# A one-layer decoder trunk on one core: gather from centred rows, refills in row pieces, and the last normalisation split between the final block's tokens and all others

## The reference, cut to what matters

```python
x = LN(alpha*x + h)                      # 1: after the mixer
x = LN(alpha*x + MemCrossAttn(x, mem))   # 2: input of router and experts
x = LN(alpha*x + MoE_top4of32(x))        # 3: the output

def layer_norm(x, g, b):
    mu = mean(x); var = mean(square(x - mu))
    return (x - mu) * rsqrt(var + LN_EPS) * g + b

logits = x @ router_w + router_b         # 32 experts, the best 4 of each token
gate = softmax(top 4 logits)
expert(x) = clamped_swiglu(x @ w_gate[e] + b_gate[e], x @ w_up[e] + b_up[e]) @ w_down[e] + b_down[e]
y[token] += gate * expert(x[token])
```

## Time and profile before

| | us |
|---|---|
| median of 3 runs | 1213.64 |
| lowest, highest | 1211.48, 1213.74 |
| the profiled execution, its own time | 1215.79 |
| its span | 1213.8 |
| PE, DVE, ACT, POOL busy in it | 1058.9, 315.2, 187.9, 24.3 |
| moved from memory | 445.0 MB, mean 368 GB/s over the span |

### The profile page before, as it was taken

One profiled execution on the slowest core, in us unless ns is written; L12 is line 12 of the kernel. 1 busy time (PEld: TensorE's weight loads), 2 busy tenths in 40 slices (PEclk: granted clock), 3 DMA queues, 4 the chain that ended last, 5 costly groups with the idle time before them and its releaser, 6 DMA issues.

```text
span 1213.8 us, 19629 instructions
## 1 busy us (share of the span) xinstructions
PE 1058.9 (87%) x7607; PEld 488.7 (40%) x7608; DVE 315.2 (26%) x993; ACT 187.9 (15%) x434; POOL 24.3 (2%) x34
## 2 busy tenths in 40 slices
PE   9999999999879889989797979796969696978786
PEld 7776874964423333323232323232323232323232
DVE  1757433212412212222121212122112121212122
ACT  0221431120111111111010101111101010101012
POOL 0110010100000000000000000000000000000000
PEclk9999999999889999999898989898989898989898
DMA  9743240587799999999999999999999999999996
GB/s 349 278 165 139 71 173 9 209 339 328 302 430 431 427 432 430 433 431 433 431 432 432 432 431 432 432 427 437 424 438 431 431 432 431 431 430 431 431 425 281
DMA packets 34953, 446.40 MB, mean 368 GB/s; under 512 B 5920, under 2 KB 6384, under 8 KB 19184
## 3 DMA queue, kind: packets, MB, share of 16 engines
q1 hardware_dynamic: 31040, 442.30, 86.3%
q10 hardware_dynamic: 3888, 3.76, 0.9%
HBM read 445.00 MB, written 1.05 MB: 367 GB/s over the span
## 4 chain that ended last, share of the span: by engine, by line
PE 50%; DMA 41%; DVE 4%; issue 2%; DVEq 1%; ACTq 1%; ACT 1%; POOLq 0%; SPq 0%; POOL 0%; PEldq 0%
DMA main<-in_exp_w_down_dram 41%; PE bank L1585 12%; PE bank L1648 10%; PE bank L1021 5%; PE bank L1031 5%; PE bank L1415 2%; PE bank L1335 2%; PE bank L1487 2%; PE bank L1627 1%; PE bank L1104 1%; PE bank L1577 1%; ACTq L919 1%; DVEq L2166 1%; DVE kst L2172 1%; DVE main L2159 1%
## 5 line engine op out<-in xcount | busy, mean ns | idle before, releaser
L1585 PE MATMUL bank<-main 128*32 128x512 f32 x3008 | 360.7, 633 | 106.8 <-DMA main<-in_exp_w_up_dram 96.5
L1585 PEld LDWEIGHTS bank<-main 128*32 128x32 f32 x3008 | 112.6, 116 | 350.7 <-issue 345.4
L1648 PE MATMUL bank<-main,kst 128*32 128x512 f32 x1504 | 181.7, 598 | 30.9 <-DMA main<-in_exp_w_down_dram 18.9
L2159 DVE TENSOR_TENSOR main<-bank,main 128x256 f32<-128x256 f32 x94 | 39.6, 422 | 550.3 <-PE bank L1627 550.3
L1532 PE MATMUL bank<-main 64*128 64x512 f32 x384 | 95.6, 615 | 0.8 <-ACT main L969 0.8
L944 ACT ACTIVATE main<-bank 128x512 f32<-128x512 f32 x46 | 27.5, 598 | 418.5 <-PE bank L1585 418.1
L1648 PEld LDWEIGHTS bank<-main,kst 128*32 128x32 f32 x1504 | 40.4, 109 | 105.0 <-issue 79.2
L1031 PE MATMUL bank<-main 128*128 128x512 f32 x176 | 77.0, 593 | 0.0
L1021 PE MATMUL bank<-main 128*128 128x256 f32 x288 | 63.5, 380 | 0.0
L1021 PEld LDWEIGHTS bank<-main 128*128 128x128 f32 x288 | 54.3, 190 | 7.6 <-issue 0.3
L1487 PE MATMUL bank<-main,kst 128*32 128x256 f32 x752 | 53.0, 394 | 2.0 <-DVE kst L2063 2.0
(11 more groups left out here) (325 smaller groups left out, 768.0 us busy)
## 6 DMA issues: line engine op xcount, KB each, us to landing
main<-in_exp_w_up_dram SPq DMA_DIRECT2D x28, 4096.0 KB, 33.3
main<-in_exp_w_down_dram SPq DMA_DIRECT2D x28, 4096.0 KB, 38.6
main<-in_exp_w_gate_dram SPq DMA_DIRECT2D x36, 2048.0 KB, 26.0
main<-in_exp_w_gate_dram SPq DMA_DIRECT2D x14, 4096.0 KB, 40.8
main<-in_exp_w_up_dram SPq DMA_DIRECT2D x7, 2048.0 KB, 14.8
main<-in_exp_w_down_dram SPq DMA_DIRECT2D x7, 2048.0 KB, 13.8
main<-in_w_in_dram SPq DMA_DIRECT2D x5, 2048.0 KB, 22.9
main<-in_w_in_dram SPq DMA_DIRECT2D x8, 512.0 KB, 9.8
```

The costliest lines, as they stand in the source:

```text
L1585: last = pe.matmul(gu_bank[at:at + CAP, :], xg_chunk(k), hidden, start=(k == 0), stop=(k == KC - 1))
L1648: last = pe.matmul(y_bank[at:at + CAP, :], hT[:, j, f, :], row(role, j)[:, h * HALF:(h + 1) * HALF], start=(f == 0 and pair == 0), stop=(f ...
L2159: return tt(dst, gT[:, :, w, :, :], b.unsqueeze(3).broadcast_to([P, 4, 2, CAP]), ALU.add)
```

## The change

**Routing.** The router's products are turned: the router weights stand still in four groups of 32 columns and the tokens move (`rp0`, `rp1`), ACT copies the four partial sums, and one product with `router_pick` adds them (`logits`). Products of the identity with itself (`stay_busy`, written into banks not yet in use) are put between the waits. The first gather no longer takes normalised rows: rows 0 to 127 are centred, multiplied by the gain and by the root, rows 128 to 255 only centred and multiplied by the gain, with the root in the selection's weight (`spread_weight`); the shift `ln_b` is put in first by a product of ones (`gathered_shift`). The shift is added to `x3` later (`ln_ready` 3 and 4), and the four `begin_sum` come after the first block's gate and up products. The table of the order is computed ahead of `gate_up`.

**Refills.** D1 of position 1 comes in three pieces, each as soon as what lies under it is used: rows 2 and 3 after the router's products (`rp1`), row 0 when the last half is centred (`centred_ready` 3), row 1 after `ln_ready` 4. `G0` and `U0` of position 2 come in two pieces of two rows, the first after step 1 of `gate_up` (`rows_used`), the second after step 3.

**The end.** While the final block's weights arrive, the rows are normalised as if the final block added nothing (`base_rows` on DVE: statistics, eight passes over 128x512), with the root set to zero for rows that have a token in the final block (`kept`). For those tokens, at most 32, the closed sums are gathered into a 64x512 tile (`gather_rows`, one half of the columns in partitions 0 to 31, the other in 32 to 63), the block's result is added there with its gate multiplied in beforehand (`gated`, one more product of 128x256 on DVE), the statistics are taken on that tile and joined by two small products (`half_mean`, `half_gap`), the tile is scaled, and PE scatters it onto the sums, which have been opened with the normalised rows. What is left for the 256 rows is a copy out of PSUM. The gains of normalisation 3 are loaded as four rows of 2 KB and spread over the partitions by PE and ACT (`spread_gain`) instead of two broadcast loads.

PE's order near the first `gate_up`, before: L1474 and L1475 are the last of the counts, L1446 opens the second sum, L1487 is the gather, L1493 its transpose, L1585 `gate_up`, L1506 to L1510 the table.

The diff, cut to its core:

```diff
+            def load_rows(role, e, odd, first, n, arrived):
+                w = d[ROLE_INPUT[role]][0].rearrange("e (p h j) n -> e h p (j n)", h=2, j=4)
+                h = (0, 0, 1, 1, 0, 1)[role]
+                cols = slice(first * D_MODEL, (first + n) * D_MODEL)
+                at = weights_at(role, odd) + first * D_MODEL
+                src = w[bass.ds(e, 1), h, :, cols].rearrange("e p n -> p (e n)")
+                sp.dma_start(main[:, at:at + n * D_MODEL], src).then_inc(arrived, 16)
...
-            sp.wait_ge(ln_ready, 5)
-            load_role(D1, 1, odd=True)
+            sp.wait_ge(unit_filled, UNIT_AT["rp1"] + 1)
+            load_rows(D1, 1, True, 2, 2, ld_d1[0])
+            sp.wait_ge(centred_ready, 3)
+            load_rows(D1, 1, True, 0, 1, ld_d1[1])
             sp.wait_ge(order_ready, 1)
...
+            def refill_first():
+                done = blocks_through(0)
+                e = expert_at(0, 2)
+                sp.wait_ge(rows_used, done)
+                for i, role in enumerate((G0, U0)):
+                    load_rows(role, e, False, 0, 2, ld_refill[i])
+                sp.wait_ge(ln_ready, 4)
+                load_rows(D1, 1, True, 1, 1, odd_full[D1])
+                sp.wait_ge(gu0_used, done)
+                for role in (G0, U0):
+                    load_rows(role, e, False, 2, 2, ring_full[ROLE_SLOT[role]])
+                sp.wait_ge(gu_done, done)
+                load_role(G1, e, odd=False)
+                load_role(U1, e, odd=False)
+                sp.wait_ge(d0_used, done)
+                load_role(D0, e, odd=False)
+                sp.wait_ge(y_done, done)
+                load_role(D1, e, odd=False)
...
+            load_gain_rows()
             load_even(N_EXPERTS - 4, 2)
             load_halves(N_EXPERTS - 4, 3, odd=True, last=True)
-            sp.wait_ge(gu0_used, blocks_through(N_EXPERTS - 2))
-            sp.dma_start(ln3_g, d["ln3_g"][0:1, :].partition_broadcast(P)).then_inc(ld_ln, 16)
-            sp.dma_start(ln3_b, d["ln3_b"][0:1, :].partition_broadcast(P)).then_inc(ld_ln, 16)
...
+                for i in range(4):
+                    b, h = divmod(i, 2)
+                    act.wait_ge(sums_closed, i + 1)
+                    act.activation(x3[:, b, h * HALF:(h + 1) * HALF], acc[b][h][:, :], ACT.Copy).then_inc(sums_copied, 1)
+                for i in range(4):
+                    ps, h = (xgT_bank, xg_bank)[i % 2], i % 2
+                    act.wait_ge(spread_done, i + 1)
+                    if i < 2:
+                        act.activation(slot_gain[32 * h:32 * h + 32, :], ps[32 * h:32 * h + 32, :], ACT.Copy)
+                    act.activation((ln3_g, ln3_b)[i // 2][:, h * HALF:(h + 1) * HALF], ps[:, :], ACT.Copy).then_inc(gain_copied, 1)
...
             def route(ps, b, steps):
                 for k in steps:
-                    last = pe.matmul(ps[:, 0:N_EXPERTS], x2T[b][:, k, :], router_w3[:, k, :], start=(k == 0), stop=(k == KC - 1))
+                    c = k % 4
+                    last = pe.matmul(ps[32 * c:32 * c + 32, 0:P], router_w3[:, k, :], x2T[b][:, k, :], start=(k < 4), stop=(k >= 4))
                 return last
+            def logits(b):
+                need(f"rp{b}")
+                pe.matmul(begin(f"rt{b}")[:, 0:N_EXPERTS], router_parts[:, b, :], router_pick,
+                          start=True, stop=True).then_inc(unit_filled, 1)
...
+            route(begin("rp0"), 0, range(0, 8)).then_inc(unit_filled, 1)
             used_up(1, "wo3")
+            bank_rp1 = begin("rp1")
+            need("x2T2")
+            route(bank_rp1, 1, range(0, 4))
             need("wo3")
...
+            logits(0)
+            stay_busy(begin("rt1"), 2)
             pe.wait_ge(x2T3_first, 1)
-            route(ps, 1, range(4, 6))
+            route(bank_rp1, 1, range(4, 6))
             need("x2T3")
-            route(ps, 1, range(6, 8)).then_inc(unit_filled, 1)
...
+            bank_xg0 = begin("xg0")
+            pe.wait_ge(ld_ln, 64)
+            gathered_shift(bank_xg0)
+            stay_busy(begin("xgT0"), 2)
             pe.wait_ge(chosen, 1)
...
+                def gather_rows():
+                    for b in range(TB):
+                        for h in range(2):
+                            pe.wait_ge(sums_copied, 2 * b + h + 1)
+                            last = pe.matmul(xgT_bank[32 * h:32 * h + 32, :], selw[:, b, :], x3[:, b, h * HALF:(h + 1) * HALF],
+                                             start=(b == 0), stop=False)
+                    last.then_inc(rows_gathered, 1)
...
+                pe.wait_ge(y_copied, n + 1)
+                pe.wait_ge(gselT_ready, n + 1)
+                scatter(0, final=True)
+                scatter(1, final=True)
+                pe.wait_ge(ld_gain, 64)
+                spread_gain(0)
+                spread_gain(1)
+                for i in (2, 3):
+                    pe.wait_ge(gain_copied, i - 1)
+                    spread_gain(i)
+                pe.wait_ge(odd_full[G0], 8 * N_EXPERTS)
+                pe.wait_ge(odd_full[U0], 32)
+                for k in range(4):
+                    gate_up(k)
+                pe.wait_ge(gain_copied, 4)
+                gather_rows()
+                pe.wait_ge(gsel_ready, n + 1)
+                for b in range(TB):
+                    pe.matmul(gselT_bank[:, 256:256 + CAP], ones, gated[:, b, :], start=(b == 0), stop=(b == 1))
+                for b in range(TB):
+                    last = pe.transpose(gselT_bank[:, b * P:(b + 1) * P], gsel_rows[:, b, :], ident)
+                last.then_inc(gselT_done, 1)
...
+                pe.wait_ge(hT_ready, n + 1)
+                pe.wait_ge(odd_full[D0], 32)
+                for f, j in [(0, j) for j in range(4)] + [(1, 0), (1, 1)]:
+                    if f == 1 and j == 0:
+                        pe.wait_ge(last_down[0], 16)
+                    for h in range(2):
+                        last = down(y_bank, 64 * h + CAP * (j % 2), f, j, h, f == 0 and j < 2, f == 1)
+                last.then_inc(y_done, 1)
+                pe.wait_ge(last_down[1], 16)
+                for h in range(2):
+                    down(xgT_bank, 32 * h, 1, 2, h, False, False)
+                pe.wait_ge(y_copied, n + 2)
+                pe.matmul(xgT_bank[0:64, :], slot_pick, y_sb, start=False, stop=False)
+                pe.wait_ge(last_down[2], 16)
+                for h in range(2):
+                    last = down(xgT_bank, 32 * h, 1, 3, h, False, True)
+                last.then_inc(slot_sums, 1)
+                reopen(2)
+                pe.wait_ge(slot_stats, 1)
+                pe.matmul(gu_bank[0:64, 0:2], half_mean, slot_mv, start=True, stop=True)
+                pe.matmul(gu_bank[0:64, 2:4], half_gap, slot_mv, start=True, stop=True).then_inc(halves_joined, 1)
+                reopen(3)
+                pe.wait_ge(slot_ready, 1)
+                for b in range(TB):
+                    for h in range(2):
+                        rows = slice(32 * h, 32 * h + 32)
+                        pe.matmul(acc[b][h][:, :], gselT[rows, b * P:(b + 1) * P], slot_z[rows, :],
+                                  start=False, stop=True).then_inc(scat_done, 1)
...
-            stt(x3[:, 0, :], x3[:, 0, :], rstd_fin[0], ln_b, ALU.mult, ALU.add).then_inc(ln_ready, 1)
+            ts(x3[:, 0, :], x3[:, 0, :], rstd_fin[0], None, ALU.mult).then_inc(centred_ready, 1)
...
+            dve.wait_ge(unit_filled, UNIT_AT["x2T3"] + 1)
+            centre_half(0)
+            dve.wait_ge(chosen, 2)
+            ts(spread_weight, M3[:, 1, 0:1], rstd_fin[1], None, ALU.mult)
+            centre_half(1)
+            dve.drain()
...
+                dve.wait_ge(gain_copied, 4)
+                dve.wait_ge(rows_gathered, 1)
+                for b in range(TB):
+                    for h in range(2):
+                        x, g, _ = halves(b, h)
+                        stt(x, x, mv_fin[b][:, 0:1], g, ALU.subtract, ALU.mult)
+                for b in range(TB):
+                    dve.wait_ge(var_out, 9 + b)
+                    tt(rstd_fin[b], rstd_fin[b], kept[:, b:b + 1], ALU.mult)
+                dve.drain()
+                for b in range(TB):
+                    for h in range(2):
+                        x, _, shift = halves(b, h)
+                        stt(x, x, rstd_fin[b], shift, ALU.mult, ALU.add).then_inc(base_ready, 1)
...
+                    tt(by_slot, by_slot, gselT_bank[:, 256:256 + CAP].unsqueeze(1).broadcast_to([P, 8, CAP]), ALU.mult)
...
+            dve.wait_ge(slot_sums, 1)
+            slot_bn = bn[0:64, 0:6]
+            dve.bn_stats(slot_bn, xgT_bank[0:64, :])
+            dve.drain()
+            dve.bn_aggr(slot_mv, slot_bn)
+            dve.drain()
+            dve.sem_inc(slot_stats, 1)
+            dve.wait_ge(halves_joined, 1)
+            joined = gu_bank[0:64, 0:4]
+            ts(slot_rstd, joined[:, 2:3], joined[:, 2:3], joined[:, 1:2], ALU.mult, ALU.add)
+            dve.drain()
```

(8 more changed lines are left out.)

366 lines of the change are left out of this document (181 added, 185 removed).

## The result

The changed kernel takes 1215.36 us (median of 9 runs, 1214.34 to 1216.55), the kernel before 1211.50 us beside it (9 runs, 1210.89 to 1213.74). The ratio is 1.0024, 95% interval 1.0015 to 1.0034: slower by about a quarter of a per cent. The forecast was 1208.9 us, faster, with 1206.3 to 1212.3 as its range. The time lies outside it, on the side to which it gave 0.08.

The account below looks back on a forecast made before the run. The constant-rate weight stream was taken to bound the kernel; only its beginning and what follows its last byte could move. The median 1213.64 less 4.7 us (start 3.3, end 1.4) gave 1208.9 us, range 1206.3 to 1212.3.

Parts of the forecast that it names:

- third sign of being wrong: At the end: the forecast is wrong if the last rows are ready later than 33.5 us after the anchor.
- the anchor: The copy ending the block before the last, at 1177.32 in the profile read; the end's times count from it.
- Part 1: Routing and first refill: refill issued 4.5 us earlier, weight stream shifted by 3.3 us, bounds 1.5 to 4.5.
- So this wait is hidden: Table ahead of the first `gate_up`: DVE's counts, some 2.3 us, are done about when the gathered tokens are ready.
- The price of D1's row 1: Refills: this row waits for the shift on DVE, and its 0.52 MB take 1.2 us off the 4.5 gained.
- The clock weighed by a rule: Routing: if the products between waits are too few, half clock stays and the shift is 1.2 instead of 3.3 us.
- Part 2: Final block, last normalisation and stores: the end of the kernel comes 1.4 us earlier, bounds 4 earlier and 2 later.
- The fourth spread ends near 1183.7: Final block: PE's scatters and gain spreads, the last two waiting for ACT's copies, are done at that time.
- the first half of `gate_up` at full clock (3.5): Final block: these products take 3.5 us after the spreads and end at 1187.2; before, they took 5.34.
- PE held at half clock between the gains' copies: Rival, final block: half clock throughout costs 11 us more, giving 1219.9 us; decides from 7.1 us on; chance 0.08.
- This is the bound, not PE: Final block: DVE's eight passes and roots, 6.5 us, set the activation's start, 0.8 us later than before.
- The last store takes 2.5 in both: Kernel end: the last store takes 2.5 us in the old and the changed kernel alike.

Follow-up runs that it names:

- the second profile: The kernel before, unchanged, profiled once more: 1211.62 us, span 1209.6 us.
- start_only: The kernel before with only the routing and refills of the change: 1213.31 us, ratio 1.0004 to the kernel before.
- gate_first: The changed kernel with the final block's first half of `gate_up` ahead of the last two gain spreads: 1212.65 us, ratio 1.0001 to the kernel before.
- warm_spreads: The changed kernel with sixteen unread 128x128 products put between the gain spreads: 1216.68 us, ratio 1.0036 to the kernel before.
- refill_whole: The kernel before with the change's routing and refills, but all refill pieces issued behind `gate_up`'s fourth step: 1215.27 us, ratio 1.0024.
- start_counts: The kernel before with the change's routing and refills, and the table behind `gate_up`'s first step: 1212.02 us, ratio 0.9999.
- first profile of before: The kernel before, unchanged, in the profile that the prediction read: span 1213.8 us, profiled execution 1215.79 us.
- the reordered end: The kernel before with the changed end, `gate_up`'s first half before the last spreads, spreads in another bank: 1211.46 us, then 1210.17 us when timed again.
- tail_only: The kernel before with only the end of the change: 1213.70 us, ratio 1.0019 to the kernel before.
- warm_start: The changed kernel with eight identity products put before the table of block counts: 1216.27 us, ratio 1.0030 to the kernel before.
- counts_second: The changed kernel with the table of block counts behind `gate_up`'s first step: 1213.98 us, ratio 1.0014 to the kernel before.

## Why the prediction was wrong, step by step

**The base.** It summed against an execution of 1213.8 us of span and a median of 1213.64. Beside more runs the median was 1211.5. 2.1 us of the miss are in that alone: the same change taken from 1211.5 would have been forecast at 1206.8, and the miss of the change itself is larger than it looks, +3.9 us measured against -4.7 forecast. The prediction's own third sign of being wrong came true: the last rows were ready 36.2 us after the anchor (1208.78 - 1172.55), and its limit was 33.5.

**Part 1, the refill 4.5 us earlier: the term that failed.** The times forecast for the changed kernel's steps came out within half a microsecond. Taken from the second profile's base (2.1 us earlier), the logits were forecast at 305.5 and read at 305.31, the selection was to end at 309.0 and ended at 308.66, the gather was to start at 309.1 and started at 308.71, and the refill was to go out at 314.3 and went out at 314.74. Two steps on the way were wrong and cost little here. "So this wait is hidden" was not so (1.37 us for DVE's counts), and `gate_up` started at 312.59 and not at 312.1. And the issue was set by the stored order and SP's 1.7 us behind it, which the prediction has no term for; the end of step 1 would have allowed 314.4. What failed is the other side of the subtraction. 320.94 held 2.1 us of half clock that a usual execution does not have. The gain in issue time is 316.72 - 314.74 = 2.0 us. The price of D1's row 1 (1.2) stands, and 0.8 is left, with 0.65 measured. The bounds of 1.5 to 4.5 had the clock in them, but only as something that the change could lose, never as something that the kernel before could have had all along. (The lower one is too high by its own terms: 3.3 less 0.7 for the logits and 1.8 for the clock is 0.8.)

**The clock weighed by a rule.** The prediction asked whether the products put between the waits are enough. In one profile they were (the changed kernel's, 1.00). In four with the same PE order and the same wait (`start_only`, `gate_first`, `warm_spreads`, `refill_whole`) they were not (0.50 from about 312), and in the three of them with the refill in pieces the anchor is 1.0 to 1.8 us behind the kernel before instead of 0.65 ahead. The Trainium skill ("TensorE: Matmul & The Clock Gate", Part 1) says that the throttled state is the default and that activity releases it. At the same gap to 0.02 us these traces show both outcomes. The same part calls the warm-up "run-variable" between runs of one kernel. These traces show that the fall in the middle of a kernel varies as well: the clock has to be priced as a chance, not as a yes or no.

**Part 2, the end 1.4 us earlier: two steps failed.** "The fourth spread ends near 1183.7", 6.4 after the anchor: it ended 8.1 after it, since PE waited 1.15 us for ACT and the second pair, 1.13 us of products, took 3.29 with its own wait and the half clock. And "the first half of `gate_up` at full clock (3.5)": it took 5.37. Together 3.6 us of the 3.8 by which the down products were late (24.6 against 20.8). The rival "PE held at half clock between the gains' copies" named this mechanism and place, and was mis-sized: it was priced at half clock throughout and decided only from 7.1 us on, because it was set against a gain of 4.7 that wasn't there. With the true start it decides from 0.65 + 1.4 + 2.4 = 4.5 us on: it cost 3.8, and the last store (below) 1.0 more. "This is the bound, not PE", said of DVE's eight passes, was also wrong: at the activation PE's transposes came last, with 0.17 us of DVE idle.

**What was right.** The way from the last down product to the last rows: 6.0 us (1202.75 to 1208.78) against 7.0 forecast and 9.7 before. The stream's line, which follows the refill one to one: the first wait on the up weights ends at 422.24, and at 422.84 in the second profile of before. No wait by "issue" at the final block.

**The last store.** "The last store takes 2.5 in both": it took 3.5, from the last rows to the end of the span. The last rows in the changed kernel and in the second profile of before:

```profile
1208.09 0.69 DVE L2386 COPY main<-bank 128x512 f32<-128x512 f32 x1 [0.17 <-PE bank L1798]
```

```profile
1205.70 1.42 DVE L2199 SCALAR_TENSOR_TENSOR main<-main,small 128x512 f32<-128x512 f32 x2 [0.51 <-POOL small L674]
```

In the kernel before one half of the output leaves early. Now all four stores become ready within 1 us, and the 1.05 MB flow at the end. Stretches of the changed kernel, and of the second profile of before:

```profile
1208.00:1209.00 1.00, 0.01 (x2) 0.00 (x0) 0.69 (x1) 0.60 (x1) 0.00 (x0) 1.00 0.32 121
1209.00:1210.00 1.00, 0.00 (x0) 0.00 (x0) 0.00 (x0) 0.00 (x0) 0.00 (x0) 1.00 1.03 381
1210.00:1211.00 1.00, 0.00 (x0) 0.00 (x0) 0.00 (x0) 0.00 (x0) 0.00 (x0) 1.00 1.02 387
```

```profile
1205.00:1206.00 1.00, 0.00 (x0) 0.00 (x0) 0.49 (x2) 0.00 (x0) 0.60 (x1) 0.70 0.70 262
...
1208.00:1209.00 1.00, 0.00 (x0) 0.00 (x0) 0.00 (x0) 0.00 (x0) 0.00 (x0) 0.50 0.75 285
```

**The sum as it is.** Refill 2.0 earlier, D1's row 1.2 later, so the anchor 0.65 earlier. From anchor to down +5.2, from down to the last rows -2.9, the last store +1.0: +3.35. In all +2.7 by the profiles, and the ratio of 1.0024 is 2.9 us. The medians differ by more, 3.9, since five of the nine executions lie at 1215.36 or above. That these are the ones in which the clock falls during the routing is argued from `start_only` and `gate_first`: no profile of the changed kernel fell on its upper level. The mean granted clock over the span agrees (0.949 to 0.951 in the four highest, 0.952 or 0.953 in the other five), but in `start_only` it does not part the levels.

**Still open.** Why the clock falls in one execution and not in the next at the same idle time, and why the end is 0.4 us longer in `start_only`, `start_counts` and `refill_whole` (36.8 against 36.4 from the anchor) though its work there is the old one. The 0.4 us lie behind the last rows (2.9 against 2.5 to the end of the span). A version without D1's late row wasn't tried: its buffer is in use until the shift is added.

## What to carry to other kernels

When a change is to win back a delay, look first whether the delay is in every execution: compare the span of the profile with the fastest of the runs, and take a stretch at half clock as a property of that execution until a second profile shows it again. When PE has to wait for another engine's copies, put products that are needed anyway into the wait; dummy products kept the clock in both runs here and cost what it was worth. And of several conditions for an issue (rows used, the order stored), price each way to its end, also the 1.7 us in which SP reads a number and issues.

## What the runs showed of the hardware

- The same idle times on PE left the clock at 1.00 in one execution and took it to 0.50 in others: 0.41, 0.51 and 1.37 us of waiting between 308.3 and 312.2 in the changed kernel, 0.41, 0.51 and 1.35 in `start_only`.
- The clock also falls where no wait shows. In the first profile of before and the first of the reordered end it fell at 307.5 and 305.8, with PE shown as busy for the whole of every microsecond from 303 on; in the second profiles of both kernels the same products left it at 1.00.
- The second pair of products with one row as the operand (`1*128 1x512`, L1717) follows a wait of 1.15 us in all four profiles with the changed order at the end and no products put into it (the changed kernel, `tail_only`, `warm_start`, `counts_second`). In all four the clock fell: just before that pair in the changed kernel (at about 1177.3, the pair starts at 1177.40) and in `tail_only`, within it in the other two (at about 1179.9 in `counts_second`, where it starts at 1177.90).
- A product of 128x128 in float32 is two records and 0.26 us (eight took 2.05 us in `warm_start`).
- Four stores of 262 KB, ready together, left at 381 to 387 GB/s in the changed kernel's two full stretches; two pairs, one issued 2.2 us behind the other, left at 240 to 285 GB/s in the second profile of before.
